# The first weight piece of a float32 decoder trunk in two halves, and one warm-up product less

## What is computed

```python
def reference(x, ...):
    h = x
    for layer in range(DEPTH):                     # 2
        xn = rms_norm(h, norm_mix_g[layer])        # h * rsqrt(mean(h^2) + eps) * g
        proj = xn @ ab_w_in[j]                     # layer 0: 1024 x 2560; pool part, q, k, v
        ...                                        # pooling, attention, output projection
        h = h + mix
        hn = rms_norm(h, norm_ffn_g[layer])
        h = h + (silu(hn @ ffn_w_gate[layer]) * (hn @ ffn_w_up[layer])) @ ffn_w_down[layer]
    return rms_norm(h, norm_final_g)
```

## Time and profile before

| | |
|---|---|
| runs | 565.61, 565.23, 565.62 us (median 565.61) |
| profiled execution | 565.88 us, its span 563.6 us |
| TensorE busy | 556.9 us, 99% of the span, 2949 products |
| DVE, ACT, POOL busy | 82%, 58%, 3% |
| DMA | 105.65 MB, mean 187 GB/s |
| chain that ended last | TensorE 98%, DVE 1%, issue 1% |

### The profile page before, as it was taken

How to read it: one execution, slowest core, us unless ns; L and a number is a source line. 1 busy time by engine, 2 the same in 40 slices (tenths; PEclk the granted TensorE clock), 3 DMA queues, 4 the chain that set the end, 5 groups by cost and what they waited for, 6 DMA issues and landing times.

```text
span 563.6 us, 7597 instructions
## 1 busy us (share of the span) xinstructions
PE 556.9 (99%) x2949; PEld 476.2 (84%) x2949; DVE 461.7 (82%) x571; ACT 325.1 (58%) x454; POOL 15.5 (3%) x55
## 2 busy tenths in 40 slices
PE   9999999999999999999999999999999999999995
PEld 8899978888888888888888888888888888888884
DVE  5669996786988879887796998977779888798775
ACT  5776864654664565555566356546475545555632
POOL 1200001000000000000000000000000000000000
PEclk9999999999999999999999999999999999999998
DMA  8975644464627384557479622445744465926321
GB/s 284 412 259 164 211 149 136 163 204 172 223 76 247 130 297 148 174 199 262 152 246 313 205 93 74 163 140 168 268 169 139 148 225 169 303 94 213 126 105 74
DMA packets 30419, 105.65 MB, mean 187 GB/s; under 512 B 3376, under 2 KB 4272, under 8 KB 30384
## 3 DMA queue, kind: packets, MB, share of 16 engines
q1 hardware_dynamic: 30240, 105.04, 54.2%
q10 hardware_dynamic: 144, 0.14, 0.1%
HBM read 104.11 MB, written 1.05 MB: 187 GB/s over the span
## 4 chain that ended last, share of the span: by engine, by line
PE 98%; issue 1%; DVE 1%; POOLq 0%; POOL 0%; DVEq 0%
PE bank L1764 20%; PE bank L1766 20%; PE bank L1765 20%; PE bank L2198 13%; PE bank L2201 7%; PE bank L1864 4%; PE bank L1867 2%; PE bank L1810 1%; PE bank L1814 1%; PE bank L1817 1%; PE bank L1836 1%; PE bank L1760 1%; PE bank L1956 1%; PE bank L2243 1%; PE bank L1982 0%
## 5 line engine op out<-in xcount | busy, mean ns | idle before, releaser
L1060 DVE TENSOR_TENSOR w_lo<-raw,w_hi 128x2048 fp32r<-128x2048 f32 (+2 forms) x91 | 203.2, 2238 | 31.3 <-ACT w_hi L585 31.3
L585 ACT ACTIVATE w_hi<-raw 128x2048 fp32r<-128x2048 f32 (+2 forms) x82 | 152.5, 1871 | 27.7 <-DMA raw<-in_slabs 25.5
L1764 PE MATMUL bank<-w_lo,yT_hi 128*128 128x512 f32 (+1 forms) x242 | 95.7, 395 | 0.0
L1766 PE MATMUL bank<-w_hi,yT_lo 128*128 128x512 f32 (+1 forms) x242 | 94.0, 388 | 0.0
L1765 PE MATMUL bank<-w_hi,yT_hi 128*128 128x512 f32 (+1 forms) x242 | 93.9, 388 | 0.0
L2198 PE MATMUL bank<-xT,w_hi 128*128 128x512 f32 x320 | 80.2, 392 | 0.0
L2198 PEld LDWEIGHTS bank<-xT,w_hi 128*128 128x128 f32 x320 | 58.0, 189 | 10.8
L1764 PE MATMUL bank<-w_lo,xT 128*128 128x512 f32 (+1 forms) x160 | 61.9, 387 | 0.0
L1766 PE MATMUL bank<-w_hi,xT 128*128 128x512 f32 (+1 forms) x160 | 60.8, 380 | 0.0
L1765 PE MATMUL bank<-w_hi,xT 128*128 128x512 f32 (+1 forms) x160 | 60.6, 379 | 0.0
L1766 PEld LDWEIGHTS bank<-w_hi,yT_lo 128*128 128x128 f32 x242 | 45.4, 188 | 9.6
(11 more groups left out here) (233 smaller groups left out, 841.9 us busy)
## 6 DMA issues: line engine op xcount, KB each, us to landing
raw<-in_slabs SPq DMA_DIRECT2D x168, 512.0 KB, 4.7
spare<-in_slabs SPq DMA_DIRECT2D x16, 512.0 KB, 5.4
raw<-in_slabs SPq DMA_DIRECT2D x6, 256.0 KB, 5.3
early<-in_slabs SPq DMA_DIRECT2D x2, 512.0 KB, 8.6
h<-in_x SPq DMA_DIRECT2D x2, 512.0 KB, 7.3
early<-in_norm_ffn_g SPq DMA_DIRECT2D x2, 512.0 KB, 6.7
raw<-in_slabs SPq DMA_DIRECT2D x4, 128.0 KB, 5.1
h<-in_x_cols SPq DMA_DIRECT2D x1, 512.0 KB, 5.7
```

The costliest lines, as they stand in the source:

```text
L585: A(w_hi[:, s % SLOTS, c], raw_of(r, c), ACT.Copy).then_inc(hi_ready, 1)
L1060: V.tensor_tensor(w_lo[:, s % SLOTS, c], raw_of(preps[s][0], c), w_hi[:, s % SLOTS, c].bitcast(F32), ALU.subtract).then_inc(lo_ready, 1)
L1764: T.matmul(o, st_hi, mv_lo, start=first, stop=False)
L1766: return T.matmul(o, st_lo, mv_hi, start=False, stop=last)
```

## The change

The first transfer is split: columns 0 to 255 of slab 0's first piece get a transfer and a semaphore of their own (`first_half_loaded`), columns 256 to 511 keep `first_loaded[0]`. ACT rounds the first half by itself (`first_half_hi`) and the second half in the place of the old piece. DVE makes `xT_hi` of column block 0 in two instructions, one for each half of the tokens. TensorE's first two products become four of 256 columns: first half of the columns for both row halves, then the second half for both. The last line takes one call from the warm-up. DVE's `w_lo` of piece 0 stays one instruction of 512 columns.

```diff
+        first_half_loaded, first_half_hi = sem("first_half_loaded"), sem("first_half_hi")
...
                 for p in range(FIRST_PARTS):
-                    c = slice(p * 512, (p + 1) * 512)
+                    if p == 0:
+                        sp.dma_start(raw[:, 0, 0:256], slabs[0, :, 0:256]).then_inc(first_half_loaded, 16)
                     for s in range(FIRST_SLABS):
+                        if s == 0 and p == 0:
+                            c = slice(256, 512)
+                        else:
+                            c = slice(p * 512, (p + 1) * 512)
                         sp.dma_start(raw[:, s, c], slabs[s, :, c]).then_inc(first_loaded[FIRST_PARTS * s + p], 16)
...
-                c = slice(p * 512, (p + 1) * 512) if s < FIRST_SLABS else slice(0, SLAB // 2)
+                c = slice(p * 512 + (256 if s == p == 0 else 0), (p + 1) * 512) if s < FIRST_SLABS else slice(0, SLAB // 2)
...
             A(lam_t[:, 0:1], power[:, 0:1], ACT.Copy)
+            act.wait_ge(first_half_loaded, 16)
+            A(w_hi[:, 0, 0:256], raw[:, 0, 0:256], ACT.Copy).then_inc(first_half_hi, 1)
...
-                        V.tensor_scalar(xT_hi[:, :, 0, :], x_in[0].rearrange("p (n t) -> p n t", n=HALVES), gcol[:, 0:1],
-                                        None, ALU.mult).then_inc(col0_hi, 1)
-                        dve.wait_ge(col0_hi, 1)
+                        for half in range(HALVES):
+                            V.tensor_scalar(xT_hi[:, half, 0, :], x_in[0][:, half * P:(half + 1) * P], gcol[:, 0:1],
+                                            None, ALU.mult).then_inc(col0_hi, 1)
+                        dve.wait_ge(col0_hi, 2)
...
-                        if u == 0:
-                            pe.wait_ge(*((cols_hi, k) if k else (col0_hi, 1)))
-                        split_done(part_hi, hi_ready, t, k)
-                        for half in range(HALVES):
-                            T.matmul(bank[:, b0 + half, :], xT_hi[:, half, k, :], w1, start=k == 0, stop=False)
+                        if u == 0 and k == 0:
+                            pe.wait_ge(first_half_hi, 1)
+                            for half in range(HALVES):
+                                pe.wait_ge(col0_hi, half + 1)
+                                T.matmul(bank[:, b0 + half, 0:256], xT_hi[:, half, k, :], w1[:, 0:256], start=True,
+                                         stop=False)
+                            split_done(part_hi, hi_ready, t, k)
+                            for half in range(HALVES):
+                                T.matmul(bank[:, b0 + half, 256:512], xT_hi[:, half, k, :], w1[:, 256:512], start=False,
+                                         stop=False)
+                        else:
+                            if u == 0:
+                                pe.wait_ge(cols_hi, k)
+                            split_done(part_hi, hi_ready, t, k)
+                            for half in range(HALVES):
+                                T.matmul(bank[:, b0 + half, :], xT_hi[:, half, k, :], w1, start=k == 0, stop=False)
...
-            keep_warm(9)
+            keep_warm(8)
```

## The result

The changed kernel takes 566.28 us (median of 22 runs, 565.82 to 566.75), the kernel before 565.40 us (22 runs, 564.98 to 565.80). The ratio is 1.0015 with a 95% interval of 1.0010 to 1.0021: 0.88 us slower, where a gain of 0.13 us was forecast and 566.2 us was the upper end of the range.

The account below looks back on a forecast made before the run. Bound: the first real product's start plus unbroken TensorE work behind it. Head start -0.15 and narrower products +0.02 sum to -0.13 us, the added issue taken as 0; from the median 565.61 to 565.5 us, range 565.0 to 566.2.

Parts of the forecast that it names:

- Part 1: Warm-up: one pair less ends it at 4.61 instead of 5.04 us, so the first product gains at most 0.43 us.
- Part 2: ACT's rounding of the first piece: first half lands about 3.8 us, takes 0.42; two halves cost 0.21 us more.
- Part 3: DVE's first column in two halves: first at 4.75, both about 5.02 instead of 4.83 us; later delay covered by 0.25.
- Part 4: First product's start: the column is its last input; head start 0.28 us, between 0.17 and 0.43, nothing if columns land later.
- the good end of the sum: Start of the first product: columns land earlier behind a first SP transfer half as long, head start 0.43 us.
- Part 5: Head start before the clock's rise: each microsecond is worth 0.53 us, so 0.28 us gain 0.15 (0.09 to 0.23).
- Part 6: TensorE's first products: four of 256 columns instead of two of 512 cost 0 to 0.03 us, taken as 0.02.
- Part 7: One more issue on SP's queue: later landings slide 0 to 0.43 us, slab 0's second piece has 0.58 cover; cost 0.
- no gain left: Rival: columns land no earlier, or the slide takes the second piece's cover and up to 0.2 us more; about 565.7; 31%.
- later rise of the clock: Rival at TensorE's start: each 512-column product still slow costs 0.20 us; twelve give 567.9 us; 6%.

Follow-up runs that it names:

- e1: The kernel before with eight warm-up calls instead of nine, nothing else; 565.37 us.
- e8: The kernel before with one added 1 KB transfer at the head of SP's queue, no data transfer split; 566.29 us.
- e2: The kernel before with only the first transfer split in two of 256 columns, ACT waiting for both and rounding 512 at once; 566.14 us.
- e4: The kernel before with the first transfer split by partitions, 64 and 64, so rows stay 2 KB; 566.41 us.
- e12: The changed kernel with the second pieces of slabs 0 and 1 rounded from the first pieces' data; 565.82 us.
- e5: The kernel before with column block 1 issued from ACT's queue, behind the first columns; 566.00 us.
- e16: The changed kernel with the first transfer whole and the second pieces rounded from the first pieces' data; 565.04 us.
- e13: The kernel before with the second pieces of slabs 0 and 1 rounded from the first pieces' data; 565.32 us.
- e3: The changed kernel with the first transfer whole again, all other parts of the change kept; 565.44 us.
- e18: The kernel before, unchanged, profiled again in one run; 565.29 us.
- e7: The changed kernel with its new transfer, the first 256 columns, issued from ACT's queue behind the first columns; 567.07 us.
- e14: The changed kernel with a 1 KB transfer ahead of the first columns on ACT's queue; 566.06 us.

## Why the prediction was wrong, point by point

Part 1 held: 16 warm-up records, no cost (e1). The bound drawn from it, 0.43 us, was too small, since the hole of 0.16 us in front of the first product closes as well; the head start is 5.20 - 4.63 = 0.57 us in the changed kernel.

Part 2 held: ACT's first half starts at 3.39, before the 3.8 I had taken, and costs 0.42 us.

Part 3 held: DVE makes both halves of the first column from 3.56 in 0.48 us, 0.13 more than before, and nobody waits for it.

Part 4: I put the column's landing between 4.42 and some tenths earlier. It came at 3.5, and the good end of the sum was the right one. The Trainium skill's rule on rings ("DMA: Bandwidth & Descriptors", section Queues, rings and completion order) pointed to that end, and the landing agrees. But the shorter rows, which the prediction gave as the reason, are not needed for it. DVE's first work on the columns, in the changed kernel and in e8, whose first data transfer is whole, with rows of 2 KB:

```profile
3.56 0.48 DVE L1096 TENSOR_SCALAR xT<-rows 128x128 fp32r<-128x128 f32 x2 [2.57 <-DMA rows<-in_x_cols]
...
3.17 0.35 DVE L1090 TENSOR_SCALAR xT<-rows 128x256 fp32r<-128x256 f32 x1 [2.18 <-DMA rows<-in_x_cols]
```

What the two share is a smaller first transfer on SP's queue. In five executions with one (changed, e2, e4, e8, e12) DVE starts on the columns at 3.17 to 3.62 us; in the twelve whose first transfer on SP's queue is the whole piece it is 4.21 to 4.51. And I left out the other side: what one queue is handed sooner, the other gets later. In e5 slab 1's first piece, the second transfer of SP's queue, was rounded 1.8 us later for a transfer on ACT's queue.

Part 5 is right only where TensorE's work sets the start of k = 1. Worked out for 0.28 us, the gain was 0.15; without the arrival (e16 against e13) k = 1 starts 0.12 us earlier in the traces and the median is 0.28 lower, in sets of times that overlap. The size is borne out at best roughly. With the arrival it is nothing (e3). The step took the earlier trace rows, "no waits", for "no wait is near".

Part 6 held: the four products of 256 columns start at 4.63 (worked out), 4.84, 5.05 and 5.27, at 0.213 us each, so they cost nothing over two of 512.

Part 7 is the step that failed, twice. Its slide, "0 to 0.43 us" for the second piece, measured 0.8 to 1.1 us (rounded from 8.41 for 7.56, 7.59 and 7.32): I let an issue slot cost what the issue takes. And its cover, 0.58 us, was read from an execution whose clock rose late; in e18 there is none and TensorE waits 0.4 us. (By its own numbers TensorE asks at 8.65 - 0.15 = 8.50 and not 8.51, so there was no margin left even on paper.) Cost: forecast 0, measured 0.88 us in the median, with the gain of part 5 gone as well. Both numbers stood on one profiled execution, and the cover on a quantity, the moment of the rise, that I myself had listed as a rival.

Of the rivals, "no gain left" named the right place, the second piece against its cover, but allowed 0.2 us beyond the cover and so ended at 565.9. The later rise of the clock wasn't what happened: worked out as in the prediction, from the starts at 5.48 and 5.78, the rise came near 5.65 us in the changed kernel's profiled execution, earlier than in the earlier trace rows. From the small spread of the times of before I had concluded that the rise hardly moves. That inference fails: where the rise is early, TensorE runs into the arrival of the second piece, and the time doesn't show it.

## What to carry to other kernels

A kernel's first microseconds are a race between transfers, and an added transfer at the head of a queue is paid by everything behind it, here with about twice its issue time (0.88 us for 0.43); count the landing of the next pieces, not the first. A wait list without entries from one execution says nothing about how near the next wait is: where the pace of an engine changes between executions, look at more than one before calling a gap cover. Where the second step already waits for its data, an earlier start of the first is worth nothing.

## What the runs showed of the hardware

TensorE's rise from 1.2 to 2.4 GHz isn't tied to the kernel. In the kernel before it came at 7.2, before 5.24 and near 5.9 us in three executions (in the second, the second and third product of 512 columns start at 5.24 and 5.48). In e7, after a hole of 0.70 us in front of the first product, products of 512 columns are still 0.43 us apart (two in 0.85) until 9.54 us, and the last row is the start of k = 1:

```profile
6.55 1.05 PE L1833 MATMUL bank<-w_hi,xT 128*128 128x512 f32 x2
7.41 1.05 PE L1836 MATMUL bank<-w_lo,xT 128*128 128x512 f32 x2
8.26 1.05 PE L1829 MATMUL bank<-w_hi,xT 128*128 128x512 f32 x2
9.11 0.86 PE L1833 MATMUL bank<-w_hi,xT 128*128 128x512 f32 x2
9.81 0.63 PE L1836 MATMUL bank<-w_lo,xT 128*128 128x512 f32 x2
10.28 0.62 PE L1829 MATMUL bank<-w_hi,xT 128*128 128x512 f32 x2
```

That the count of slow products differs between executions of one kernel is what the Trainium skill ("TensorE: Matmul & The Clock Gate", Part 1) says, and these runs agree. A hole alone doesn't decide it: e8 has one of 0.42 us in front of its first product, and its products of 512 columns start at 5.81 and 6.04, 0.23 us apart. The granted clock column read 1.00 from 1 to 9 us in the traces of before, of the changed kernel, of e8 and of e14, while the spacing changed.

A 1 KB transfer ahead of SP's others delays the next pieces by 0.44, 1.27 and 0.79 us (e8 against the first trace of before; the last by 0.5 against the other two), though its own issue takes 0.4. An issue on SP's queue took 0.37 to 0.50 us in most cases, and 0.56 to 0.58 for the first three of e4.
